# A decoder step on one core: the head norm's Newton steps go to GpSimd, and normalising goes one step later

## What is computed

```python
def head_norm(o, g):                       # on the retention output, per row and head
    mu = jnp.mean(of, axis=-1, keepdims=True)
    var = jnp.mean((of - mu) ** 2, axis=-1, keepdims=True)
    y = ((of - mu) * lax.rsqrt(var + EPS)).reshape(B, T, H * dv)

def mla_sample(q_lat, q_pe, ckv_new, kpe_new, pool_ckv, pool_kpe, page_table):
    ckv_past = pool_ckv[page_table].reshape(DB, -1, KV_LORA)
    s_past = einsum('bqhc,bkc->bhqk', q_lat, ckv_past) + einsum('bqhr,bkr->bhqk', q_pe, kpe_past)
    p = softmax(...)
    return einsum('bhqk,bkc->bqhc', p[..., :P], ckv_past) + ...

def mem_attend(q, mk, mv):                 # prompt rows on 256 memory rows, 4 heads of 128
    p = softmax(einsum('bthd,bmhd->bhtm', q, mk) * MEM_SCALE)
    return einsum('bhtm,bmhd->bthd', p, mv)
```

## Time and profile before

| | us |
|---|---|
| median of 3 runs | 2654.25 (2649.67 to 2656.87) |
| the profiled execution, its own time | 2648.21 |
| its span, first to last instruction | 2646.4 |
| PE busy over the span | 2322.0 (88%) |
| DVE busy | 1257.6 (48%) |
| ACT busy | 632.4 (24%) |
| POOL busy | 135.7 (5%) |

### The profile page before, as it was taken

How to read it: one execution, slowest core, us unless ns; L and a number is a source line. 1 busy time by engine, 2 the same in 40 slices (tenths; PEclk the granted TensorE clock), 3 DMA queues, 4 the chain that set the end, 5 groups by cost and what they waited for, 6 DMA issues and landing times. The chain is left out here.

```text
span 2646.4 us, 49914 instructions
## 1 busy us (share of the span) xinstructions
PE 2322.0 (88%) x21131; PEld 1911.2 (72%) x21131; DVE 1257.6 (48%) x3012; ACT 632.4 (24%) x1407; POOL 135.7 (5%) x149
## 2 busy tenths in 40 slices
PE   5489999999999957599999898488999999959998
PEld 2389999998888845467677676366776777748886
DVE  1711344211111024299999997465545443345554
ACT  0410122110101000033333333133333333331110
POOL 0000000000000000122222221000000000000000
PEclk8589999999999975599999999699999999979999
DMA  4322233221111161499999995210000000064442
GB/s 167 122 67 73 76 107 93 67 77 61 70 69 49 40 217 33 181 384 366 367 377 370 358 380 200 79 40 29 27 20 20 20 7 11 5 205 151 159 163 68
DMA packets 139922, 355.62 MB, mean 134 GB/s; under 512 B 15072, under 2 KB 84576, under 8 KB 131512
## 3 DMA queue, kind: packets, MB, share of 16 engines
q0 software_dynamic: 22976, 185.35, 18.4%
q1 hardware_dynamic: 116736, 167.25, 18.4%
HBM read 289.09 MB, written 63.46 MB: 133 GB/s over the span
## 5 line engine op out<-in xcount | busy, mean ns | idle before, releaser
L529 PE MATMUL pj_ps<-pj_wh,pj_xh 128*128 128x256 f32 (+1 forms) x1152 | 326.1, 283 | 7.1 <-DVE pj_wl L466 7.1
L529 PE MATMUL pj_ps<-pj_wl,pj_xh 128*128 128x256 f32 (+1 forms) x1152 | 325.9, 283 | 0.0
L529 PE MATMUL pj_ps<-pj_wh,pj_xl 128*128 128x256 f32 (+1 forms) x1152 | 325.9, 283 | 0.0
L1412 DVE STREAM_TRANSPOSE sa_turned<-sa_nat 128x2048 f32<-128x2048 f32 x128 | 293.4, 2293 | 22.8 <-DMA sa_kp<-cache_kpe,sa_index 22.6
L499 DVE TENSOR_SCALAR pj_stage<-pj_ps 128x256 f32<-128x256 f32 (+2 forms) x72 | 38.6, 536 | 499.3 <-PE pj_ps L526 301.9
L1640 PE MATMUL sa_ps_s<-sa_turned,sa_q 128*32 128x128 f32 x5120 | 184.6, 278 | 52.8 <-DVE sa_turned L1412 46.9
L529 PEld LDWEIGHTS pj_ps<-pj_wh,pj_xh 128*128 128x128 f32 x1152 | 222.3, 193 | 7.4 <-DVE pj_wl L466 7.2
L529 PEld LDWEIGHTS pj_ps<-pj_wl,pj_xh 128*128 128x128 f32 x1152 | 222.3, 193 | 0.0
L529 PEld LDWEIGHTS pj_ps<-pj_wh,pj_xl 128*128 128x128 f32 x1152 | 222.2, 193 | 0.0
L746 DVE CUSTOM_DVE_ANT_0 la_row<-la_ps_s,la_causal 128x512 f32<-128x512 f32 (+3 forms) x160 | 97.6, 611 | 232.6 <-PE la_ps_s L887 230.7
L526 PE MATMUL pj_ps<-pj_xh,pj_wh 128*128 128x512 f32 x512 | 199.3, 389 | 0.0
(11 more groups left out here) (336 smaller groups left out, 3994.0 us busy)
## 6 DMA issues: line engine op xcount, KB each, us to landing
pj_raw<-w_in POOLq DMA_DIRECT2D x16, 1024.0 KB, 5.9
s_zn<-pj_stage SPq DMA_DIRECT2D x64, 256.0 KB
s_zt<-pj_stage SPq DMA_DIRECT2D x32, 512.0 KB
rm_z<-s_zn SPq DMA_DIRECT2D x16, 768.0 KB, 9.5
mg_cat<-s_cat SPq DMA_DIRECT2D x16, 768.0 KB, 6.3
mg_gate<-s_zt SPq DMA_DIRECT2D x16, 768.0 KB, 8.0
pn_x<-x_prompt SPq DMA_DIRECT2D x4, 2048.0 KB, 8.4
mg_x<-x_prompt SPq DMA_DIRECT2D x16, 512.0 KB, 4.1
```

The source lines that it names most:

```text
L529: mm = pe.matmul(ps[:, n % QUAD, 0:w], x[:, k, u * P:(u + 1) * P], wt[:, j, k, 0:w], **flags)
L1412: dve.transpose(turned[:, s, a:z, :, :].rearrange("p c x q -> p x c q"), of.rearrange("p x (c q) -> p x c q", q=QR)).then_inc(t_ok, 1)
```

## The change

- On DVE the two instructions of the guess stay (`guess_ok`). The three Newton steps and the shift move to POOL, as 14 instructions on 128 x 4 numbers: 4 for each step in place of 3, and 2 for the shift in place of 1. Each waits for the one before through a semaphore (`newton`).
- POOL does them (`roots`) ahead of its DMAs of step 4b+7, in program order.
- ACT normalises a step later, after `memory_out` and ahead of `copy_probs`. `retention_out` goes to the end of the same step.
- PE turns the normalised retention a step later, after `values` and ahead of the next block's memory scores. The next block's queries and keys are turned after its memory scores, where they were turned between the second and third piece of scores.
- DVE's statistics wait for the last block's roots.

```diff
+        guess_ok, newton = m.sem("guess_ok"), m.sem("newton")
@@ gpsimd
+                link = linker(pool, newton)
+
+                def roots(b):
+                    pool.wait_ge(guess_ok, b + 1)
+                    for _ in range(3):
+                        link(pool.tensor_tensor(tmp[:, :], root[:, :], root[:, :], ALU.mult))
+                        link(pool.tensor_tensor(tmp[:, :], tmp[:, :], var[:, :], ALU.mult))
+                        link(pool.tensor_scalar(tmp[:, :], tmp[:, :], -0.5, 1.5, ALU.mult, ALU.add))
+                        link(pool.tensor_tensor(root[:, :], root[:, :], tmp[:, :], ALU.mult))
+                    link(pool.tensor_tensor(shift[:, :], mean_var[:, :, 0], root[:, :], ALU.mult))
+                    pool.tensor_scalar(shift[:, :], shift[:, :], -1.0, None, ALU.mult).then_inc(root_ok, 1)
+
                 pool.wait_ge(index_ok, 1)
-                for g in range(STEPS):
+                for g in range(STEPS + 4):
+                    if begun(g, 7) is not None:
+                        roots(begun(g, 7))
+                    if g >= STEPS:
+                        continue
                     if g >= DEEP:
 
                         pool.wait_ge(pv_ps, g - DEEP + 1)
@@ vector
                 def head_statistics(b):
+                    if b >= 1:
+                        dve.wait_ge(root_ok, b)
@@
-                    inverse_root(dve, link, var[:, :], root[:, :], tmp[:, :])
-                    dve.scalar_tensor_tensor(shift[:, :], mean_var[:, :, 0], -1.0, root[:, :], ALU.mult, ALU.mult)\
-                       .then_inc(root_ok, 1)
+                    link(dve.tensor_scalar(tmp.bitcast(I32)[:, :], var.bitcast(I32)[:, :], 1, None, ALU.logical_shift_right))
+                    dve.tensor_scalar(root.bitcast(I32)[:, :], tmp.bitcast(I32)[:, :], -1.0, float(0x5F3759DF), ALU.mult, ALU.add)\
+                       .then_inc(guess_ok, 1)
@@ scalar
                     if begun(g, 4) is not None:
                         memory_out(begun(g, 4))
-                        retention_out(begun(g, 4))
+                        normalise(begun(g, 4))
                     if 1 <= g <= STEPS:
                         copy_probs(g - 1)
...
                     if begun(g, 3) is not None:
                         memory_turned(begun(g, 3), 1)
-                        normalise(begun(g, 3))
+                    if begun(g, 4) is not None:
+                        retention_out(begun(g, 4))
@@ tensor
                         scores(g, 1)
-                    if begun(g, 0) is not None:
-                        turn_queries_keys(begun(g, 0))
...
                         values(g - 1)
+                    if begun(g, 4) is not None:
+                        turn_retention(begun(g, 4))
                     if begun(g, 0) is not None:
                         memory_scores(begun(g, 0))
+                        turn_queries_keys(begun(g, 0))
...
                         memory_values(begun(g, 3))
-                        turn_retention(begun(g, 3))
```

## The result

The changed kernel takes 2714.91 us (median of 6 runs, 2700.41 to 2722.24) against 2651.96 before on the same chips: 1.0229 times as long by the comparison of the runs, 95% interval 1.0194 to 1.0263, which is some 61 us (the two medians lie 63 apart). It was forecast slower, at 2688.

A forecast was written before the change was run, and what follows sets the result against it. DVE, 95% busy, was taken to set the pace, with PE and the DMAs close behind. Per block -1.97 + 4.0 + 0.5 - 0.4 = +2.1, times 16 +34 us: 2682, and 6.0 for the median makes 2688; range 2650 to 2740.

The forecast's parts named there:

- What DVE saves: On DVE, the Newton steps and shift leave between guess and next transpose: 1.97 us saved in each block.
- When POOL starts: On POOL, the roots stand behind the two DMAs of step 4b+6, so they begin 5 us after the guess.
- What an instruction costs there: On POOL, each of the 14 chained instructions takes 0.30 us, the chain 4.2 us.
- What waits for it: Normalising, copy, `values` and memory scores follow the roots, so DVE's `memory_top` waits 4.0 us a block.
- What is later behind it: PE turns the next queries and keys after the memory scores, so DVE's `new_low` waits another 0.5 us a block.
- DVE's waits for DMAs vanish: On DVE, the waits for the cache's DMAs vanish in a longer block: -0.4 us a block.
- The ISA row: On POOL, a row once ahead of the first root, put at 0, at most a few us once.
- A: Rival: POOL's steps are cheap, below 0.09 us each, and the saving stands: -24 us, 2630; chance 0.12.
- B: Rival: the saving is given back to PE or the DMAs, time stays about 2652; chance 0.10.
- C: Rival: POOL is much slower, 0.5 us and more an instruction: +78 us, 2732; chance 0.20.
- D: Rival: the clock falls through PE's new hole in each block, adding 1 to 2 us a block, 2710; chance 0.08.

The follow-up runs named there:

- the last experiment: Changed kernel with roots sooner on POOL, normalising right behind `exp`, retention turned before the second scores, latents half loaded: 2611.1 us, 31.6 below the kernel before, likewise halved.
- the repaired one: Changed kernel with roots ahead of the DMAs of step 4b+6, normalising right behind `exp`, retention turned ahead of the second piece of scores: 2647.59 us, ratio 0.9994.
- the order alone: Changed kernel with the roots back on DVE, keeping the new order of ACT and PE: 2678.64 us, ratio 1.0086 to the kernel before.

## Why the prediction was right, and where its size was off

- *What DVE saves*: 1.97 us a block. Right; the guess at 1406.52 is followed by the transpose at 1406.60, and the last experiment returned 31.6 us against 31.5. That the two agree so closely is luck, as the intervals are wider.
- *When POOL starts*: right. The roots stand 4.85 us after the guess. POOL's 0.30 after a DMA issue isn't there ahead of an arithmetic instruction (1411.34 to 1411.37).
- *What an instruction costs there*: 0.30 taken, 0.28 measured (1411.37 to 1411.65; 0.20 and a gap of 0.08), the chain 3.86 for 4.2. By the Trainium skill's ratio (GPSIMD Engine Reference, section 3.1) it would have been 0.386, which these rows don't bear out: on 4 floats, where the page has 2048, the ratio to VectorE's spacing of 0.197 is 1.42.
- *What waits for it*: right in kind; in size partly by luck. From the first root to `memory_top` I had 1323.90 - 1313.44 = 10.46 us; the block above shows 9.99. I had 4.0 us of DVE's wait at `rm_bias`; it fell on two places, `sa_acc` and `rm_bias`, 32.4 + 29.5 = 61.9 us over 15 blocks, 4.1 each. I had `add_up`'s wait for `values` inside that of `memory_top`, which is the same time. But the chain and the path behind it were shorter than I had them, and a lower clock, for which the sum had no term, made up for that: behind the late `values` the two waits are 4.7 us in the mean of the ten blocks with the lower clock, and 2.1 in the five others.
- *What is later behind it*: the term that was mis-sized. I had 0.5 us at `new_low`, reckoned from PE's mean pace, and nothing at the state. They are 22.5 / 15 = 1.5 and 15.1 / 15 = 1.0 us a block. The turning of queries and keys, to which I put it, costs nothing alone. What the runs show in its place: with the retention's turn ahead of the memory scores, and `values` late, PE's own gaps grow and reach DVE. Of the 22.5 us 19.0 are seven waits of over 1 us, six of them just behind such a gap.
- *DVE's waits for DMAs vanish* (-0.4): wrong. They went from 6.7 us over 15 blocks to 9.5. The buffers come free as late as the values do, so a longer block doesn't make the loads early; that is my reading, and no run tests it.
- Summed again with what was measured: -1.97 + 4.1 + 1.5 + 1.0 + 0.2 = +4.8, less the 0.5 that the state, `memory_top` and `new_low` waited before (7.3 us over 15): +4.4 by the unrounded terms, 16 of which are 70 us. The period grew by 37.4 - 32.8 = 4.6. Both stand beside the profiled executions' difference of 74 (2722.24 to 2648.21).
- *The ISA row*, put at 0: in the first block the roots follow the DMA issue by 0.11 us (1150.73 + 0.94 to 1151.78), in the block above by 0.03. The 6 us that the Trainium skill gives for a first call after a load (GPSIMD Engine Reference, section 2.1) don't show here; whether anything was loaded at that row no run shows.
- *The rivals*: A is excluded by 0.28. B was wrong for this kernel; in the repaired one the time stayed and waits for loads took the saving, mostly those issued behind the roots. C is excluded by the same 0.28. D, which I gave 0.08, came beside the forecast and not in its place: the granted clock in the stage went from 0.99 to 0.96, and PE's matmuls took 18 us longer. D had put 1 to 2 us a block on it, and it was 1.1. No run takes the lower clock away by itself, so how much of the 18 reached the total is open; most of it lies on the chain for which DVE waits.

## What to carry to other kernels

Before a chain goes to an idle engine, find what stands ahead of it in that engine's queue, what stands behind it there, and what stands behind its consumer: here one place behind two DMA issues cost 51 us, and one place ahead of them it held those loads back. A hole that the chain tears in the matrix engine can cost twice, as the wait and as a lower clock behind it. An engine at 92% has slack only between certain instructions: half a us more in one gap came with a cost of 17 us, and a whole us elsewhere cost nothing. When three resources stand at 95, 93 and 92%, relief of the first may be worth little more than the distance to the second. Halve the second one's work to see that, and before you blame its speed look which of its transfers were merely issued late.

## What was not expected of the hardware

PE stands still for up to 3.3 us with nothing that the profile shows it waiting for, in the changed kernel about once a block (14 gaps of over 0.6 us in 15 blocks; the kernel before has 7). These gaps shrank when the loads were halved (28.5 to 10.5 us in 490), so traffic has a part in them in this kernel; before, they did not (11.8 to 13.0). That they are fetches of instructions was not shown.

The lower clock stands behind a hole of PE, but not behind every one: behind the wait of 3.2 us for the copy it came in ten of 14 blocks, and behind the waits of at most 1.1 us in the run with one Newton step in none of 15. After a gap of 2.81 us in the order alone the granted clock was at the lower of its two levels for some 3 us, though PE was busy throughout:

```profile
1402.00:1405.00 3.00, 0.19 (x2) 0.10 (x2) 1.27 (x1) 1.28 (x6) 0.00 (x0) 0.92 0.94 384
1405.00:1408.00 3.00, 3.00 (x31) 2.42 (x34) 0.28 (x3) 0.00 (x0) 0.00 (x0) 0.51 0.47 184
```

After the like gap of 2.80 us in the changed kernel it stayed at 1.00:

```profile
1427.60:1431.00 3.40, 3.37 (x56) 2.23 (x56) 1.78 (x4) 1.31 (x5) 0.00 (x0) 1.00 0.44 174
```
